# Two half-width filler products in place of each full one at the start of a two-block transformer kernel

## The chip, the core and the metric

The kernel runs on one core of one Trainium2 chip. The metric is device time in microseconds (us), the median over several executions. An execution of this kernel repeats to within half a microsecond (1849.61 to 1850.11 in three runs).

## What is computed

The reference is two transformer blocks in a row on one sequence of 256 tokens with 1024 features, all in float32. The first has a gated linear recurrence beside a latent attention, a cross attention to a memory of 256 tokens, and a gated feed-forward part. The second has a dilated and differential attention, a feed-forward part, a gated recurrent mixer (HGRN) and a mixture of eight experts of which two are chosen for each token. Only its very first step matters here:

```python
def rms_norm(x, g):
    xf = x.astype(jnp.float32)
    y = xf * lax.rsqrt(jnp.mean(xf * xf, axis=-1, keepdims=True) + EPS)
    return (y * g.astype(jnp.float32)).astype(x.dtype)
...
    h = rms_norm(x, attn_norm)
    proj = h @ w_in
```

## The kernel before

The engines' programs are written out by hand, each in one block, and meet at semaphores. The tokens lie on 128 partitions in two tiles. The weights stream from memory in units of 128 x 2048 float32 (1 MB): SyncE (SP) loads them into a ring of seven buffers `raw`, ScalarE (ACT, L1461 and L2107) rounds each to its high part `wh`, VectorE (DVE, L2225 and L3188) makes the low part `wl` as the difference, and TensorE (PE) multiplies with high and low parts (`split_product`, L425 to L436). A ring slot comes free when the low part is made; a slot of `wh` and `wl` when TensorE has used it.

The start of the program, which the change touches, goes like this.

- GpSimd (POOL) fills the tile `junk`, 128 x 512 float32, with ones (L2162) and raises `idle_columns`.
- TensorE waits for that and issues fourteen filler products (L596). Each has 128 stationary columns and 512 moving ones, all from `junk`, and writes bank 7 of `ps`. Nothing reads the result. A float32 product is run by the chip as two passes, so that the trace has 28 matmul records and 28 weight loads for the fourteen.
- In the meantime ACT sums the squares of `x` (L1481), and DVE scales its rows into `xn` (L2274), once `x` has arrived.
- TensorE then waits for `xn` and transposes it through the array (`norm`, L488), eight chunks by two tiles. ACT writes the high part of the transposed rows (L1499) and DVE the low part (L2283), both into `hT_both`. Then the first weight product starts (L425).

Every engine works strictly in the order in which its program is written: the fillers stand ahead of the transposes in TensorE's queue, ACT's rounding of weight units 1 and 2 (L1461) stands behind its part of `hT_both`, and DVE's low parts of them stand behind its own part. SP's load of the memory tokens (`mem`, L1422) waits for the transposes, and the loads of units 7 and later stand behind it.

Further on, three places of the kernel are of use for comparison. `hg_scores` (L1100) issues products with 32 or 64 stationary columns that go in turn to the lower and the upper half of the output partitions (`q0` is 0 or 64), so in turn to the two halves of the array's columns. `score` (L894, L895) issues products that contract over 32 rows only, those of successive heads in different rows of the array; at 412.5 us two heads come together, at 416.3 us one head alone. `hg_out_of` (L1134, L1140) issues products of 64 stationary columns that all go to the same half.

Of the kernel before, what the change touches and what calls it, by code (L numbers as in the profile page):

```python
# [26 lines left out]
P = 128  # L27
# [6 lines left out]
HALF = 512  # L34
# [73 lines left out]
def build(nc, units_d, consts_d, cols_d, rows_d, lru_w_d, x_d, mem_d, pos_d, out_d):  # L108
    def sb(name, shape, dt=F32):
        return nc.alloc_sbuf_tensor(name, [P] + shape, dt)  # L110
# [17 lines left out]
    junk = sb("junk", [HALF])  # L128
# [8 lines left out]
    ps = nc.alloc_psum_tensor("ps", [P, 8, HALF], F32)  # L137
# [50 lines left out]
    for shared, parts in SHARED.items():  # L188
        start = 0
# [4 lines left out]
    def sem(name):  # L194
        shared = place.get(name, (name, 0))[0]
        if shared not in sems:
            sems[shared] = nc.alloc_semaphore(shared)
        return sems[shared]
# [206 lines left out]
    def _(pe):  # L405
# [186 lines left out]


        pe.wait_ge(sem("idle_columns"), 1)
        for _ in range(14):
            nc.tensor.matmul(ps[:, 7, :], junk[:, 0:P], junk[:, 0:HALF], start=True, stop=True)  # L596
        norm("attn_norm")
        def lru_in(n, b):

# [851 lines left out]
    def _(act):  # L1451
# [352 lines left out]
        def exponentials(i):  # L1804
            _, _, _, _, _, n = score_of(i)
            act.wait_ge(*reached("dil_att_max", i + 1))
            if i >= 4:
                act.wait_ge(*reached("dil_att_transposed", (i - 4) // 2 + 1 if i < 12 else i - 7))
            p, s = apr[i % 4], asc[i % 2]
            A(p[:, 0:P], s[:, 0:P], ACT.Exp, bias=dnmax[:, n:n + 1], accum_out=dsum[:, n:n + 1])  # L1810
            A(p[:, P:], s[:, P:], ACT.Exp, bias=dnmax[:, n + 1:n + 2],
              accum_out=dsum[:, n + 1:n + 2]).then_inc(sem("dil_att_probs"), 1)
# [392 lines left out]
    def _(dve):  # L2205
# [494 lines left out]
        def biased(i):  # L2700
            _, _, _, dist, slope, n = score_of(i)
            s = asc[i % 2]
            dve.wait_ge(*reached("dil_att_scores", i + 1))
            if i >= 2:
                dve.wait_ge(*reached("dil_att_probs", i - 1))
            V.scalar_tensor_tensor(out=s, in0=dist, scalar=-slope, in1=ps[:, S_BANKS[i % 2], 0:DIST_W], op0=ALU.mult,
                                   op1=ALU.add).then_inc(sem("dil_att_read"), 1)
            dve.wait_ge(*reached("dil_att_read", i + 1))
            V.reduce_max(dnmax[:, n:n + 1], s[:, 0:P], AX, negate=True)
            V.reduce_max(dnmax[:, n + 1:n + 2], s[:, P:], AX, negate=True).then_inc(sem("dil_att_max"), 1)  # L2710
# [15 lines left out]
        def out_copied(j):  # L2726
            _, _, cs = value_of(j)
            dve.wait_ge(*reached("dil_att_weighted", j + 1))
            if j < DIFF_HEADS:
                for t in range(TT):  # L2730
                    ins = V.tensor_scalar(xn[:, t, cs], ps[:, O_BANK, 64 * t:64 * t + 64], dinv[:, 4 * j + t:4 * j + t + 1],
                                          None, ALU.mult)
            else:
                ins = V.tensor_copy(xn[:, :, cs], ps[:, O_BANK, 0:P].rearrange("p (t c) -> p t c", t=TT))
            ins.then_inc(sem("dil_att_out"), 1)
# [660 lines left out]
```

## Time and profile before

| | us |
|---|---|
| median of three runs | 1849.94 |
| lowest and highest | 1849.61, 1850.11 |
| span of the profiled execution | 1847.0 |
| first filler starts, last filler ends (TensorE) | 1.32, 15.13 |
| first transposition starts | 14.96 |

The profile is of one execution. Its span goes from the first to the last instruction on the engines. The profiled execution's own device time is not listed apart from its span; the median of the runs is 2.9 us above the span. The clock column of a stretch is TensorE's granted clock as a share of full speed, 1.00 for 2.4 GHz and 0.50 for 1.2 GHz. A matmul's duration in the records holds the way through the array, so that the time between two starts, not the duration, tells how fast passes follow each other.

### The profile page before, as it was taken

To read this page: it belongs to the slowest core of one execution; us is meant where nothing else is said; L and a number is where in the kernel's file an instruction comes from. 1 tells how busy PE (TensorE), PEld (TensorE's weight loads), DVE (VectorE), ACT (ScalarE), POOL (GpSimd) and SP (SyncE) were. 2 spreads that over 40 slices of the span, in tenths; PEclk is the share of its full clock that TensorE was granted. 3 is DMA by queue.
4 is the path that set the end of the run, shared out by engine and by line. 5 is a ranking of instruction groups with operands and counts; after the bars stand their busy time and mean duration, and the time that the engine had idled before them with its cause. 6 is when DMAs were issued, how large, how long until landed. Compare 5 with 4: busy or idle time off the path is not lost.

```text
span 1847.0 us, 24636 instructions
## 1 busy us (share of the span) xinstructions
PE 1808.2 (98%) x9274; PEld 1515.2 (82%) x9274; DVE 1502.7 (81%) x1546; ACT 1258.3 (68%) x1334; POOL 25.6 (1%) x27
## 2 busy tenths in 40 slices
PE   9989999999999999999999999999999999999997
PEld 7877788888788888987888888888888888888886
DVE  7975799568678855776988989889888889898896
ACT  6975677457655535564777777777777777777775
POOL 0000000000000000000000000000000000000000
PEclk9999999999999999999999999999999999999999
DMA  9422455543155554433799999999999999999994
GB/s 362 159 103 78 169 191 185 197 168 117 69 181 182 187 201 157 163 137 114 308 369 359 396 376 354 371 359 397 370 353 385 355 398 372 337 390 377 375 376 157
DMA packets 69087, 491.89 MB, mean 266 GB/s; under 512 B 7792, under 2 KB 8176, under 8 KB 10096
## 3 DMA queue, kind: packets, MB, share of 16 engines
q1 hardware_dynamic: 67248, 484.33, 69.0%
q0 software_dynamic: 1728, 6.03, 1.6%
q8 instruction: 76, 1.25, 0.3%
q14 instruction: 35, 0.29, 0.0%
HBM read 485.09 MB, written 5.24 MB: 265 GB/s over the span
## 4 chain that ended last, share of the span: by engine, by line
PE 90%; DVE 5%; ACT 4%; issue 1%; POOL 0%; DVEq 0%; ACTq 0%; POOLq 0%
PE ps L425 22%; PE ps L434 21%; PE ps L427 21%; PE ps L561 9%; PE ps L564 5%; PE ps L445 1%; PE ps L1381 1%; DVE wl L2225 1%; PE ps L865 1%; PE ps L866 1%; PE ps L870 1%; PE ps L436 1%; PE ps L429 1%; PE ps L1282 1%; PE ps L596 1%
## 5 line engine op out<-in xcount | busy, mean ns | idle before, releaser
L3188 DVE TENSOR_TENSOR wl<-raw,wh 128x2048 fp32r<-128x2048 f32 x334 | 761.2, 2291 | 88.2 <-ACT wh L2107 87.5
L2107 ACT ACTIVATE wh<-raw 128x2048 fp32r<-128x2048 f32 x333 | 637.9, 1918 | 182.6 <-PE ps L434 182.6
L425 PE MATMUL ps<-wh,hT_both 128*128 128x512 f32 (+2 forms) x1128 | 443.0, 394 | 5.9 <-DVE hT_both L2535 1.6
L427 PE MATMUL ps<-wh,hT_both 128*128 128x512 f32 (+2 forms) x1128 | 434.7, 386 | 0.0
L2225 DVE TENSOR_TENSOR wl<-raw,wh 128x2048 fp32r<-128x2048 f32 x124 | 283.2, 2287 | 81.8 <-ACT wh L1461 81.5
L434 PE MATMUL ps<-wl,hT_both 128*128 128x512 f32 (+2 forms) x1128 | 300.9, 386 | 0.0
L1461 ACT ACTIVATE wh<-raw 128x2048 fp32r<-128x2048 f32 x125 | 238.4, 1913 | 70.0 <-PE ps L434 68.9
L425 PE MATMUL ps<-wh,work_r 128*128 128x512 f32 x648 | 254.7, 393 | 0.0
L427 PE MATMUL ps<-wh,work_r 128*128 128x512 f32 x648 | 252.5, 390 | 0.0
L425 PEld LDWEIGHTS ps<-wh,hT_both 128*128 128x128 f32 x1128 | 212.0, 188 | 49.4 <-issue 4.5
L427 PEld LDWEIGHTS ps<-wh,hT_both 128*128 128x128 f32 x1128 | 212.1, 188 | 40.2
L434 PEld LDWEIGHTS ps<-wl,hT_both 128*128 128x128 f32 x1128 | 209.8, 188 | 42.9
L434 PE MATMUL ps<-wl,work_r 128*128 128x512 f32 x648 | 200.3, 390 | 0.6 <-DVE wl L3188 0.6
L561 PE MATMUL ps<-hT_both,wh 128*128 128x512 f32 x704 | 178.2, 394 | 2.8 <-DVE hT_both L2283 2.6
L561 PEld LDWEIGHTS ps<-hT_both,wh 128*128 128x128 f32 x704 | 126.2, 189 | 28.0 <-issue 3.0
L434 PEld LDWEIGHTS ps<-wl,work_r 128*128 128x128 f32 x648 | 121.2, 188 | 28.1 <-DVE wl L3188 2.8
L425 PEld LDWEIGHTS ps<-wh,work_r 128*128 128x128 f32 x648 | 121.7, 188 | 25.7 <-issue 1.0
L427 PEld LDWEIGHTS ps<-wh,work_r 128*128 128x128 f32 x648 | 121.7, 188 | 24.6
L564 PEld LDWEIGHTS ps<-hT_both,wl 128*128 128x128 f32 x704 | 96.1, 190 | 6.9
L564 PE MATMUL ps<-hT_both,wl 128*128 128x256 f32 x704 | 98.2, 282 | 0.0
L2117 ACT ACTIVATE work<-ps 128x512 f32<-128x512 f32 x56 | 33.5, 599 | 40.7 <-PE ps L434 40.7
L425 PE MATMUL ps<-hT_both,wh 128*128 128x256 f32 x192 | 49.2, 292 | 2.1 <-DVE hT_both L2283 2.0
(448 smaller groups left out, 1731.5 us busy)
## 6 DMA issues: line engine op xcount, KB each, us to landing
raw<-in_units SPq DMA_DIRECT2D x458, 1024.0 KB, 6.9
x<-in_x SPq DMA_DIRECT2D x2, 512.0 KB, 5.8
work<-in_lru_w SPq DMA_DIRECT2D x1, 1024.0 KB, 15.1
xn<-in_mem SPq DMA_DIRECT2D x1, 1024.0 KB, 15.6
out<-x POOLq DMA_DIRECT2D x2, 512.0 KB, 6.7
consts<-in_consts POOLq DMA_DIRECT2D x1, 768.0 KB, 5.6
consts<-in_consts SPq DMA_DIRECT2D x1, 356.0 KB, 11.5
cols<-in_cols SPq DMA_DIRECT2D x1, 202.0 KB, 2.5
```

The costliest lines, as they stand in the source:

```text
L425: nc.tensor.matmul(out, sh, mh, start=(first and j == 0), stop=False)
L427: nc.tensor.matmul(out, sl, mh, start=False, stop=False)
L429: nc.tensor.matmul(out, sh, ml, start=False, stop=False)
L434: ins = nc.tensor.matmul(out, sh, ml, start=False, stop=done)
L436: ins = nc.tensor.matmul(out, sl, mh, start=False, stop=done)
L561: nc.tensor.matmul(out, w[0][:, k, cs], hT_both[:, :, k, :], start=(k == 0), stop=False)
L564: ins = nc.tensor.matmul(out[:, 0:S], w[1][:, k, cs], hTh[:, k, :], start=False, stop=(k == KD - 1))
L1461: A(wh[:, n % SPLIT, :], raw[:, n % RAW, :], ACT.Copy).then_inc(sem("hi_made"), 1)
L2107: A(wh[:, n % SPLIT, :], raw[:, n % RAW, :], ACT.Copy).then_inc(sem("hi_made"), 1)
L2117: A(esg, ps[:, 2 * (c % 2), :], ACT.Silu).then_inc(sem("gate_silu"), 1)
L2225: V.tensor_tensor(wl[:, n % SPLIT, :], raw[:, n % RAW, :], wh[:, n % SPLIT, :].bitcast(F32), ALU.subtract).then_inc(sem("lo_made"), 1)
L3188: V.tensor_tensor(wl[:, n % SPLIT, :], raw[:, n % RAW, :], wh[:, n % SPLIT, :].bitcast(F32), ALU.subtract).then_inc(sem("lo_made"), 1)
```

## The change

Each turn of the filler loop issues two products in place of one. The first has stationary columns 0 to 63 of `junk` and writes partitions 0 to 63 of bank 7, the second has columns 64 to 127 and writes partitions 64 to 127. So each uses all 128 rows and one half of the columns of the array. The first still streams the 512 columns of `junk` in their order. The second streams the same 512 columns in another order: `by_turns` takes them alternately from the first and the second 256, that is columns 0, 256, 1, 257 and so on. All values are ones, and nothing reads the result.

```diff
         pe.wait_ge(sem("idle_columns"), 1)
+        by_turns = junk[:, 0:HALF].rearrange("p (a b) -> p b a", a=2)
         for _ in range(14):
-            nc.tensor.matmul(ps[:, 7, :], junk[:, 0:P], junk[:, 0:HALF], start=True, stop=True)
+            nc.tensor.matmul(ps[0:64, 7, :], junk[:, 0:64], junk[:, 0:HALF], start=True, stop=True)
+            nc.tensor.matmul(ps[64:P, 7, :], junk[:, 64:P], by_turns, start=True, stop=True)
         norm("attn_norm")
```

On TensorE, at the start of the program, the order before is this (a row is a line, the operation, out<-in and the output's shape; each float32 product counts once here):

```order
L404 UNCONDITIONAL_BRANCH
L596 MATMUL ps<-junk 128x512 x14
L488 MATMUL ps<-consts,xn 128x128 x16
L425 MATMUL ps<-hT_both,wh 128x256
L429 MATMUL ps<-hT_both,wh 128x256
```

And this is the beginning of it with the change:

```order
L404 UNCONDITIONAL_BRANCH
L597 MATMUL ps<-junk 64x512
L598 MATMUL ps<-junk 64x512
L597 MATMUL ps<-junk 64x512
L598 MATMUL ps<-junk 64x512
```

The pair comes fourteen times, then the sixteen transposes of L488 follow as before. No instruction of another engine, and nothing later on TensorE, is moved; later lines are numbered two higher.

## Rows read from the trace of the kernel before

**Rows 1.** The page: span, busy time by engine, and the engines' shares of the chain.

```profile
span 1847.0 us, 24636 instructions
PE 1808.2 (98%) x9274; PEld 1515.2 (82%) x9274; DVE 1502.7 (81%) x1546; ACT 1258.3 (68%) x1334; POOL 25.6 (1%) x27
...
PE 90%; DVE 5%; ACT 4%; issue 1%; POOL 0%; DVEq 0%; ACTq 0%; POOLq 0%
```

**Rows 2.** The chain that ended last, first 40 us: start, us, what.

```profile
0.74 0.54 POOL junk L2162
1.28 0.04 issue
1.32 13.81 PE ps L596 x28
15.13 0.45 PE ps L488 x4
...
15.66 3.03 ACT hT_both L1499 x8
18.70 1.81 ACT wh L1461
...
20.53 4.50 DVE wl L2225 x2
```

**Rows 3.** Timeline of DVE up to 15.4 us: start, us, engine, line, operation.

```profile
10.27 1.42 DVE L2274 TENSOR_SCALAR xn<-x,small 128x1024 f32<-128x1024 f32 x2
...
13.10 2.29 DVE L2225 TENSOR_TENSOR wl<-raw,wh 128x2048 fp32r<-128x2048 f32 x1 [1.41 <-ACT wh L1461]
```

**Rows 4.** All waits for a DMA in the whole kernel: us in total, times, longest.

```profile
DVE small L2356 <- DMA cols<-in_cols: 2.4, 1, 2.4
ACT xn L1481 <- DMA x<-in_x: 1.7, 2, 1.0
ACT wh L1461 <- DMA raw<-in_units: 1.1, 1, 1.1
```

**Rows 5.** Timeline, the fillers' weight loads (each starts with its pass) and the last filler.

```profile
2.34 0.34 PEld L596 LDWEIGHTS ps<-junk 128*128 128x128 f32 x1 [0.52 <-issue]
3.19 0.34 PEld L596 LDWEIGHTS ps<-junk 128*128 128x128 f32 x1 [0.52 <-issue]
4.05 0.34 PEld L596 LDWEIGHTS ps<-junk 128*128 128x128 f32 x1 [0.52 <-issue]
4.67 0.19 PEld L596 LDWEIGHTS ps<-junk 128*128 128x128 f32 x1 [0.28 <-issue]
5.10 0.19 PEld L596 LDWEIGHTS ps<-junk 128*128 128x128 f32 x1 [0.24 <-issue]
...
14.54 0.59 PE L596 MATMUL ps<-junk 128*128 128x512 f32 x1
14.96 0.93 PE L488 MATMUL ps<-consts,xn 128*128 128x128 f32 x7
```

**Rows 6.** Timeline of PE, 757.9 to 758.3 us: column halves in turn.

```profile
757.93 0.45 PE L1100 MATMUL ps<-work 128*32 128x32 f32 x16
```

**Rows 7.** Timeline of PE, about 412.5 and 416.3 us: two heads, then one.

```profile
412.50 0.50 PE L894 MATMUL ps<-work 32*128 32x128 f32 x4
412.82 0.60 PE L895 MATMUL ps<-work 32*128 32x256 f32 x4
413.36 0.50 PE L865 MATMUL ps<-wh,hT_both 128*128 128x512 f32 x1
...
416.34 0.48 PE L894 MATMUL ps<-work 32*128 32x128 f32 x2
416.67 0.59 PE L895 MATMUL ps<-work 32*128 32x256 f32 x2
417.19 0.39 PE L865 MATMUL ps<-wh,hT_both 128*128 128x256 f32 x1
```

**Rows 8.** Timeline of PE, 786.2 to 790 us: one half, then the whole array.

```profile
786.24 1.09 PE L1140 MATMUL ps<-work 128*64 128x128 f32 x8
787.26 0.50 PE L425 MATMUL ps<-wh,hT_both 128*128 128x512 f32 x1
...
789.21 1.07 PE L434 MATMUL ps<-wl,hT_both 128*128 128x512 f32 x4
```

**Rows 9.** Stretches: length, PE, PEld, DVE, ACT, POOL busy, granted clock, DMA share, GB/s.

```profile
866.00:870.00 4.00, 3.43 (x27) 2.15 (x25) 2.91 (x11) 3.33 (x8) 0.00 (x0) 1.00 0.74 291
...
715.00:718.00 3.00, 2.07 (x12) 1.64 (x12) 3.00 (x8) 3.00 (x7) 0.00 (x0) 0.97 0.00 0
718.00:721.50 3.50, 3.50 (x18) 3.36 (x17) 3.50 (x3) 2.80 (x6) 0.00 (x0) 0.54 0.13 23
```

**Rows 10.** Timeline of PE, 865.5 to 868.4 us: first and last of 24 eight-column products.

```profile
865.49 0.28 PE L1257 MATMUL ps<-hT_both,rh 128*8 128x256 f32 x1 [1.28 <-DVE hT_both L2283]
...
868.33 0.28 PE L1259 MATMUL ps<-hT_both,rh 128*8 128x256 f32 x1
```

## The prediction

> **What bounds the kernel now.** I read the page first: TensorE is busy for 98% of the span of 1847.0 us and holds 90% of the chain of work that ended last [rows 1]. Then I read that chain from its beginning [rows 2]. It starts with GpSimd's fill of `junk`, stays on TensorE for all 28 passes of the fillers from 1.32 us to 15.13, and goes on through the first transposes, ACT's high parts, ACT's rounding of a weight unit and DVE's low parts. So the fillers themselves are on the path. They need not be: DVE had the rows `xn` ready at 10.27 + 1.42 = 11.69 us [rows 3], and the first transpose started at 14.96, where the last filler let go [rows 5]. The fillers run about 3.3 us past the moment at which the transposes could have started. Whatever they get longer therefore delays the first transpose by the same amount, with no cover at all.
>
> Would a delay there be swallowed later? I looked for slack in the waits for DMA, since a transfer that arrives at a fixed time would absorb a shift. There are three kinds of such waits in the whole kernel, 5.2 us together, and all are over before 12 us, ahead of the first transpose [rows 4]. Behind that point every wait is of one engine for another, and all of them descend from the transposes. I take it that a shift of the first transpose reaches the end undiminished.
>
> **The change, step by step.** The loop issued 14 products, or 28 passes. It now issues 28 products of half the width, or 56 passes, and the time of a pass depends on the 512 moving columns, not on how wide the stationary part is: passes of 128 moving columns and 64 stationary ones follow each other at about (1.09 - 0.27)/7 = 0.117 us in [rows 8], where 0.27 us is the way of the last one through the array. So no half-product is cheaper than a full one. All depends on whether the two halves run at the same time.
>
> *Do the halves run together?* In [rows 6] sixteen passes of 32 moving columns go to the two column halves in turn, with different moving columns. They start (0.45 - 0.20)/15 = 0.017 us apart, again less the way through the array. By the fillers' warm rate of 0.43 us for 512 columns [rows 5], 32 columns take 0.027 us. Passes that start faster than one can stream are overlapping: one pair per 0.033 us, against 0.054 if they ran one behind the other. The row-wise counterpart is clearer, since it is longer: at 412.50 us the eight passes of two heads take 0.86 us up to the next product, and at 416.34 the four passes of one head alone take 0.85 [rows 7]. The second head is free. So I expect 28 pair-passes at the old spacing, and nothing for the doubled count.
>
> *What a pair costs beyond one pass.* The row-wise case gives 0.01 us on four pair-passes, 0.003 each. The column-wise case gives 0.033 - 0.027 = 0.006 each. I take 0.004, between the two and nearer to the row-wise one since its passes are long as the fillers are: 28 x 0.004 = 0.1 us. The ends are 0 and 28 x 0.006 = 0.17 us.
>
> *Leaving the half-width arrangement.* The full-width transposes follow directly. In [rows 8] the last half-width pass of L1140 starts at 786.24 + 1.09 - 0.27 = 787.06, and the full-width L425 starts at 787.26, 0.20 us later instead of the 0.11 that a pass of 128 columns streams. That is 0.09 us, paid once. The ends are 0 and 0.2 us, should the start of the array's new arrangement cost as much again.
>
> *The interleaved moving operand.* The second half-product reads columns 256 apart in turn, so neighbours in the stream are never neighbours in memory. No row before has such a moving operand, so I bound it. Below: nothing, or a spacing of 0.43 us per warm pass as it is. The better reason for this end is [rows 8]: the rounded weights' passes of L434 stream 512 columns every (1.07 - 0.39)/3 = 0.227 us, so contiguous elements can be delivered at nearly twice the rate at which a float32 filler pass consumes them. If jumping halves the delivery, 512 columns take 0.454 us, and the filler pass barely notices: 24 warm passes x 0.026 = 0.6 us. Above: if a float32 pass fetches its elements twice, or jumping costs more, the second half-product takes twice its time. Then a pair-pass takes 0.86 us while the clock is full, and the 24 passes from 4.67 us on give 24 x 0.43 = 10.3 us more; the first four, which ran at half clock, already have 0.85 us each. I take the lower end, nothing, since the nearest row says that the delivery has a reserve of two.
>
> The Trainium skill speaks against this step of mine. "Advanced Engine Details and Errata", section SBUF Cachelines, says that an access which goes to another 16-byte line each time pays, and that two hits on a line are wanted to hide the memory's latency. The interleaved operand never gives two hits, and the page does not say how large the penalty is; by it the sum would be somewhere from the 0.6 us to the 10.3 us above. No row here tests it. It is the first rival below.
>
> *Everything else* stays: weight loads are twice as many, but each lies beneath a pass of 0.43 us and takes 0.19 us at most with a full clock [rows 5]; the two halves write different partitions; bank 7 is read by nobody; SP, ACT, DVE and POOL have the same programs.
>
> The sum: 0.1 + 0.09 + 0 = 0.2 us. The profiled span would go from 1847.0 to 1847.2, and the median of the runs, which stands 2.9 us above the span, from 1849.94 to about **1850.2 us**, rounded up for the possible part of the interleaved operand. A measurement here can tell about 0.2%, or 3.7 us, from no change, so this is "the same". The forecast's own range is 1849.4 to 1851.5: the lower end is the scatter of the runs and a clock that happens to rise early, the upper one takes in the 0.6 us, 0.17, 0.2 and the scatter.
>
> **The rivals.**
>
> *Jumping reads are slow (chance 0.23).* Mechanism: the second product of each pair streams at half its rate, place: all warm filler passes, price 24 x 0.43 = 10.3 us, and it decides from the point at which jumping delivers less than one element in 0.84 us (0.43/512). Time 1849.9 + 10.3 + 0.2 = **1860.4, slower**. For it: the rule above, and that the one moving operand made so is new here. Against it: the reserve of two. A lesser slowing, of a third, would give 3.4 us.
>
> *The halves do not overlap at 512 columns (0.05).* Then 56 passes run one behind the other. The clock rises at the same time, so about four passes lie ahead of 4.67 us and 52 behind it: 4.67 + 52 x 0.43 = 27.0 us instead of 14.96, or +12.0, **1862**. Against it: [rows 6, 7].
>
> *The clock does not rise during half-width products (0.05).* Now it does so between the passes at 4.05 and 4.67, where the spacing falls from 0.85 to 0.43 us [rows 5]. If it stayed at half until other work comes, 24 passes would cost 0.43 us more each, 10.3 us, and the first transposes would be slow too: **1861**. Against it: 24 products with as few as 8 stationary columns, almost back to back from 865.49 to 868.33 us [rows 10], go by at a granted clock of 1.00 [rows 9]; the one drop to about half, at 718 us, follows a stretch in which TensorE stood idle for a third of the time [rows 9]. A rise later by one or two passes would cost under 1 us and stays inside "the same".
>
> *The fillers get shorter (0.02).* If the clock rose right at the first pass, the first four would save 0.43 us each, 1.7 us: 1848.2, still no more than 0.1%. For a gain beyond 3.7 us the pair would have to run faster than a single product, which no row suggests.
>
> **How the numbers follow.** The forecast has 0.65, and the small saving 0.02. The three slow rivals have 0.33 together, nearly all at +10 to +12 us. Of the jumping reads' 0.23 about 0.01 would be too small to be told from no change. Faster by over 0.2%: 0.02, the most that I leave for what I have not seen. Same: 0.66. Slower: 0.32. Since the slow cases hold a third, a range for 8 times in 10 has to reach them: it goes from 1849.2 to 1862.2. With a third of the cases at its far end, the predicted time stays that of the likeliest.
>
> **What would show it.** Right: in the new profile the fillers start at 1.32 us as before, the records of the two lines come in pairs that start a few nanoseconds apart, successive pairs 0.85 us apart at first and 0.43 from about 4.7 us on, and the first transpose starts at 15.0 to 15.3. Wrong by jumping reads: the spacing stays near 0.85 us although the granted clock is 1.00, or the second record of a pair lasts longer than the first, and the first transpose starts near 25 us. Wrong by the clock: the same spacing at a granted clock of 0.50. Wrong by missing overlap: the records of L597 and L598 start 0.43 us apart from each other, and the transposes start near 27. Wrong on the path: the transposes start late, but the span does not grow by as much.

## The result, and the profile after

The changed kernel took 1852.76 us (median of 18 runs, 1850.99 to 1853.66), the kernel before 1849.66 us (median of 18, 1847.44 to 1851.76). The ratio is 1.0018 with a 95% interval of 1.0011 to 1.0026. So the change costs about 3.1 us, which lies on the border of what I had called "the same": the interval lies above 1, so the kernel did become slower, and it reaches to both sides of my bound of 0.2%. The scatter is wider than the three first runs had suggested, some 4 us between the extremes of the kernel before and not half a microsecond.

The changed kernel's page, its first lines, beside [rows 1]:

```profile
span 1851.9 us, 24692 instructions
...
PE 1814.9 (98%) x9302; PEld 1519.0 (82%) x9302; DVE 1502.4 (81%) x1546; ACT 1258.0 (68%) x1334; POOL 25.5 (1%) x27
```

56 instructions more are the 28 additional passes and their weight loads. DVE and ACT have the same busy time as before. The place to look is the chain's beginning, beside [rows 2]; here is its piece from the end of the fillers on (start, us, what):

```profile
16.14 2.33 PE ps L598 x5
18.47 0.60 PE ps L488 x4
...
19.16 3.02 ACT hT_both L1501 x8
```

ACT's high parts start at 19.16 in place of 15.66, 3.5 us late. The links after the fillers are the same as before. The end of the fillers in the chain is five passes of L598 alone, the interleaved half. The timeline of TensorE shows how that comes about; first while the array runs at half clock, then at full clock, then at the end (start, us, what):

```profile
3.94 1.06 PE L597 MATMUL ps<-junk 128*64 128x512 f32 x1
3.95 1.05 PE L598 MATMUL ps<-junk 128*64 128x512 f32 x1
4.79 1.06 PE L597 MATMUL ps<-junk 128*64 128x512 f32 x1
4.80 1.05 PE L598 MATMUL ps<-junk 128*64 128x512 f32 x1
...
6.32 0.59 PE L597 MATMUL ps<-junk 128*64 128x512 f32 x1
6.38 0.71 PE L598 MATMUL ps<-junk 128*64 128x512 f32 x1
6.75 0.59 PE L597 MATMUL ps<-junk 128*64 128x512 f32 x1
6.92 0.71 PE L598 MATMUL ps<-junk 128*64 128x512 f32 x1
7.18 0.59 PE L597 MATMUL ps<-junk 128*64 128x512 f32 x1
7.46 0.70 PE L598 MATMUL ps<-junk 128*64 128x512 f32 x1
...
15.07 1.07 PE L597 MATMUL ps<-junk 128*64 128x512 f32 x2
15.61 2.87 PE L598 MATMUL ps<-junk 128*64 128x512 f32 x5
18.41 0.44 PE L488 MATMUL ps<-consts,xn 128*128 128x128 f32 x2
```

Three things are to be read here. At half clock the two halves start 0.01 us apart and the pairs follow each other every 0.85 us, as single products did. At full clock L597 goes on at 0.43 us from pass to pass (6.32, 6.75, 7.18), but L598 takes 0.54 (6.38, 6.92, 7.46), and it falls behind: the two halves do not wait for each other, up to a lead of four or five passes. The last two passes of L597 came 0.60 and 0.48 us after the one before, so that a limit on the lead is possible; no run tests it. At the end L597 is done (at 16.14 us) and L598 runs its last passes alone, (2.87 - 0.71)/4 = 0.54 us each. The first transpose starts at 18.41 instead of 14.96, which is 3.45 us.

The clock rose later in this execution than in the one before: the spacing falls to the full-clock value after 5.64 us instead of after 4.05. (The granted clock column reads 1.00 up to the first recorded change, so that only the spacing tells.) By the clock's own records it rose at 6.1 and 4.4 us, and 1.7 us at half speed cost 0.85 of those 3.45. About 22 full-clock passes x 0.112 = 2.5 us and 0.09 us for the way back to full width are the rest. A median over 18 runs does not hang on one execution's clock, so the slow half-product was the suspect for the 3.1 us, and there were two further candidates to clear: the sharing of the array, and the clock.

### The profile page after: what moved, and what is told of

Its sections match the earlier page's. It is cut to its first block, busy times and chain, and to the rows that moved or that the text cites. A ratio compares the mean times of both kernels' runs of the same rounds, so it can differ in the third digit from the quotient of the medians.

```text
span 1851.9 us, 24692 instructions
## 1 busy us (share of the span) xinstructions
PE 1814.9 (98%) x9302; PEld 1519.0 (82%) x9302; DVE 1502.4 (81%) x1546; ACT 1258.0 (68%) x1334; POOL 25.5 (1%) x27
## 4 chain that ended last, share of the span: by engine, by line
PE 90%; DVE 5%; ACT 3%; issue 1%; POOL 0%; DVEq 0%; ACTq 0%; POOLq 0%
PE ps L425 22%; PE ps L434 21%; PE ps L427 21%; PE ps L561 9%; PE ps L564 5%; PE ps L445 1%; PE ps L1383 1%; PE ps L867 1%; DVE wl L2227 1%; PE ps L868 1%; PE ps L872 1%; PE ps L436 1%; PE ps L1284 1%; PE ps L429 1%; ACT wh L1463 1%
## 5 line engine op out<-in xcount | busy, mean ns | idle before, releaser
L434 PE MATMUL ps<-wl,hT_both 128*128 128x512 f32 (+2 forms) x1128 | 300.9, 386 | 0.0
L434 PEld LDWEIGHTS ps<-wl,hT_both 128*128 128x128 f32 x1128 | 209.8, 188 | 42.9
L434 PE MATMUL ps<-wl,work_r 128*128 128x512 f32 x648 | 200.4, 390 | 0.5 <-DVE wl L3190 0.5
L434 PEld LDWEIGHTS ps<-wl,work_r 128*128 128x128 f32 x648 | 121.1, 188 | 28.2 <-DVE wl L3190 2.8
```

Of the source, the lines that this page charges most:

```text
L434: ins = nc.tensor.matmul(out, sh, ml, start=False, stop=done)
```

## The experiments

In all of them only the filler loop of the kernel before is edited (and nothing reads what it computes), unless said. A diff shows the whole edit against the kernel before. The comparison is with the kernel before, run on the same chip. The theories: A, the order of reading costs, whoever reads beside it; B, two streams at once starve each other; C, half-width products delay the clock's rise.

**Both halves in memory order.**

```diff
-            nc.tensor.matmul(ps[:, 7, :], junk[:, 0:P], junk[:, 0:HALF], start=True, stop=True)
+            nc.tensor.matmul(ps[0:64, 7, :], junk[:, 0:64], junk[:, 0:HALF], start=True, stop=True)
+            nc.tensor.matmul(ps[64:P, 7, :], junk[:, 64:P], junk[:, 0:HALF], start=True, stop=True)
```

> Both half-products of each pair stream the 512 columns in memory order; nothing else differs from the change. Theory A (the reading order costs: an interleaved moving operand streams 512 float32 columns in 0.54 us in place of 0.43, whoever reads beside it): both halves go at 0.43 us per pass at full clock, the first transpose starts at 15.0 to 15.3 us when the clock rises at about 4.4 us (0.43 us later for each microsecond by which it rises later), and the time is within 0.5 us of the kernel before, about 1849.9. Theory B (contention: two streams at once starve each other, whatever their order): the second half stays at 0.54 us per pass, transposes near 18, time near 1852.8. Theory C (half-width products delay the rise of the clock): the spacing falls to 0.43 only after 6 us again, and the time is about 0.9 us above the kernel before.

Measured: 1849.97 us (11 runs) against 1849.65, ratio 1.0001 (0.9992 to 1.0010). The end of the fillers in its timeline:

```profile
13.74 0.59 PE L596 MATMUL ps<-junk 128*64 128x512 f32 x1
13.74 0.59 PE L597 MATMUL ps<-junk 128*64 128x512 f32 x1
...
14.60 0.59 PE L596 MATMUL ps<-junk 128*64 128x512 f32 x1
14.60 0.59 PE L597 MATMUL ps<-junk 128*64 128x512 f32 x1
15.12 1.09 PE L488 MATMUL ps<-consts,xn 128*128 128x128 f32 x8
```

The pairs are in step, two of them in 0.86 us, as single products were. The doubled number of products is free. The transposes follow the last pair after 0.52 us where a pass takes 0.43: the way back to full width costs the 0.09 us of the forecast. A transpose at 15.12 and a span of 1847.0 us, that of the kernel before, speak against B, and C falls too, since the clock had risen by the pass at 4.72 us.

**Full-width products, interleaved.**

```diff
+        by_turns = junk[:, 0:HALF].rearrange("p (a b) -> p b a", a=2)
         for _ in range(14):
-            nc.tensor.matmul(ps[:, 7, :], junk[:, 0:P], junk[:, 0:HALF], start=True, stop=True)
+            nc.tensor.matmul(ps[:, 7, :], junk[:, 0:P], by_turns, start=True, stop=True)
```

> Fourteen full-width fillers as before, but each streams its 512 columns interleaved (0, 256, 1, 257 and so on). Theory A: 24 warm passes at 0.54 us, the first transpose about 2.6 us later than before, near 17.6, and the time about 2.7 us above the kernel before, like the changed kernel. Theory B: there is one stream only, so passes stay at 0.43 us and the time at 1849.7. Theory C: the clock rises at about 4.4 us, time as before.

Measured: 1852.49 us (9 runs) against 1849.65, ratio 1.0022 (1.0012 to 1.0032).

```profile
16.11 1.78 PE L597 MATMUL ps<-junk 128*128 128x512 f32 x3
17.73 0.82 PE L488 MATMUL ps<-consts,xn 128*128 128x128 f32 x6
```

Passes are (1.78 - 0.70)/2 = 0.54 us apart with a single stream, and the first transpose starts at 17.73, 2.77 us after that of before at nearly the same rise of the clock. So nearly the whole price of the change, 2.8 of 3.1 us in the medians, comes without any half-width product. A holds.

**Both halves interleaved.**

```diff
+        by_turns = junk[:, 0:HALF].rearrange("p (a b) -> p b a", a=2)
         for _ in range(14):
-            nc.tensor.matmul(ps[:, 7, :], junk[:, 0:P], junk[:, 0:HALF], start=True, stop=True)
+            nc.tensor.matmul(ps[0:64, 7, :], junk[:, 0:64], by_turns, start=True, stop=True)
+            nc.tensor.matmul(ps[64:P, 7, :], junk[:, 64:P], by_turns, start=True, stop=True)
```

> Both half-products of each pair stream interleaved. Theory A: both at 0.54 us per pass, in step with each other, and the same time as the changed kernel, 1852.8. Theory B or a mixture (two jumping streams meet in the same memory): a spacing above 0.54 us, up to 0.86, and a time from 1853 to 1860.

Measured: 1853.45 us (11 runs) against 1849.65, ratio 1.0018 (1.0009 to 1.0027).

```profile
6.50 1.02 PE L597 MATMUL ps<-junk 128*64 128x512 f32 x1
6.51 1.01 PE L598 MATMUL ps<-junk 128*64 128x512 f32 x1
7.36 0.70 PE L597 MATMUL ps<-junk 128*64 128x512 f32 x1
7.36 0.71 PE L598 MATMUL ps<-junk 128*64 128x512 f32 x1
7.90 0.70 PE L597 MATMUL ps<-junk 128*64 128x512 f32 x1
7.90 0.71 PE L598 MATMUL ps<-junk 128*64 128x512 f32 x1
```

Two jumping streams run in step at 0.54 us: no extra price for the second. The time alone would not have told: 1853.45 lies in the range that I had given to a mixture with B, 0.7 us above the changed kernel's median; but the ratios of the two are the same, 1.0018, and the spacing decides. At half clock, up to 6.50, the interleaved passes take 0.85 us like any other. In this execution the clock rose only at 7.35 us.

**Ten fillers, and eighteen.** Full width, memory order; `range(10)` and `range(18)` in place of `range(14)`. Ten asks whether there is a gain, eighteen whether a delay reaches the end.

> Ten full-width fillers in memory order in place of fourteen: 8 passes or 3.4 us less. Expected if the fillers stand on the path as the chain has it: they end at about 11.7 us, when the scaled rows are ready, ACT's high parts start at 13.1 (behind its rounding of the first weight unit) in place of 15.7, DVE's low parts at 15.4 (behind its low part of the first unit) in place of 16.5, and the time is 1.2 to 2.0 us below the kernel before, about 1848. Rival: a later stage absorbs the shift, and the time is as before. Rival: with fewer fillers the clock is lost again in the early products, and the time is above the kernel before.

> Eighteen full-width fillers in memory order in place of fourteen: 8 warm passes of 0.429 us, 3.43 us more ahead of the transposes, and nothing else. If a delay there reaches the end undiminished, the time is 3.4 us above the kernel before, about 1853.1, somewhat above the changed kernel, whose fillers let go 2.8 us late at the same rise of the clock. If a later stage swallows part of a delay, the time is less than 2.5 us above the kernel before, and then the changed kernel's 3.1 us must have another source than its fillers.

> The same kernel as the one with ten fillers, for a narrower interval. If it is faster at all, the two sets of runs together give a median 0.4 to 1.2 us below the kernel before; if the first difference was scatter, this one lies within 0.3 us of it.

Eighteen: 1853.01 us (11 runs) against 1849.49, ratio 1.0018 (1.0009 to 1.0027). The chain starts like this:

```profile
1.32 17.14 PE ps L596 x36
...
19.00 3.03 ACT hT_both L1499 x8
```

3.43 us of plain fillers in order, and 3.5 us at the end. The delay arrives undiminished, within the scatter. The changed kernel's 3.1 us agree with the delay of about 2.8 us in its fillers; the interval of the ratio, 2.0 to 4.8 us, can't tell the two apart.

Ten: 1848.91 us (11 runs) against 1849.65, and again 1848.63 (11 runs) against 1849.83, both times with a ratio of 0.9995 (0.9986 to 1.0004). Both medians are lower, by 0.7 and 1.2 us, and both intervals reach above 1, so that neither set by itself excludes no change. The 22 executions together have a median of 1848.85 us, against 1849.65 of the 45 of the kernel before that were measured beside them: 0.8 us less, which lies in the 0.4 to 1.2 that I had named for a real gain. By the means it is 1.0 us with a standard error of 0.3, if each execution counts as independent. So a small gain is likely, and it is smaller than the 1.2 to 2.0 us expected at first.

One reason is in the chain, which no longer holds the fillers. In the first profile it goes over the transfer of a weight unit, ACT's rounding and DVE's low part of it (start, us, what):

```profile
3.10 8.51 DMA raw<-in_units
```

Four fillers less end 3.43 us earlier, but less of that can be gained, since the first weight unit is now what is waited for. In this execution the clock also rose late, at 7.4 us, the first transpose started at 13.02 us and ACT's high parts at 13.72, 1.9 us earlier than before, yet its span is 1848.0 us. Another reason is visible in the stretches (length, PE, PEld, DVE, ACT, POOL busy, granted clock, DMA share, GB/s):

```profile
13.00:17.60 4.60, 2.74 (x22) 2.32 (x21) 4.03 (x6) 4.42 (x10) 0.00 (x0) 1.00 1.02 425
17.60:21.00 3.40, 3.40 (x17) 3.40 (x17) 3.40 (x5) 2.75 (x2) 0.00 (x0) 0.51 1.00 424
21.00:25.00 4.00, 4.00 (x35) 4.00 (x35) 3.79 (x10) 0.80 (x3) 0.00 (x0) 0.99 1.01 426
```

TensorE ran 3.4 us at half clock and gave part of the gain back. The stretch ahead of it, with TensorE busy for 2.74 of 4.60 us, does not explain that: in the second profile of the same kernel it was busy for less, and no such drop followed.

```profile
13.00:17.60 4.60, 2.19 (x17) 1.72 (x14) 4.52 (x7) 4.60 (x10) 0.00 (x0) 1.00 1.01 423
```

The clock had risen at 5.3 us there, and the span was 1848.0 us as well, with four half-clock stretches of 3.4 us further on, where the profile of the kernel before has one. What makes them come is open.

**Eight fillers**, `range(8)`.

> Eight full-width fillers: 12 passes or 5.1 us less than before. They end at 9.9 to 11.3 us, ahead of the scaled rows at 11.7, so that the transposes start at about 11.9. The chain then goes over ACT's rounding of the first weight unit, which lasts to 13.1 us: ACT's high parts start there at the earliest, as with ten fillers. Expected 1.0 to 2.0 us below the kernel before, no better than ten fillers. Rival: the shorter warm stretch makes half-clock stretches in the first products likelier, each of 3.4 us costing up to 1.7 us, and the time is that of the kernel before or above.

Measured: 1848.89 us (11 runs) against 1849.49, ratio 0.9995 (0.9986 to 1.0004). The transposes start at 11.69 us, released by `xn`. The clock rose at 6.9 us and fell to half from 17.1 to 20.5, as in the first profile of ten. A small gain is possible and not shown, and none of these versions beats the kernel before clearly.

**Which orders cost.** Full-width float32 fillers: five in memory order, then two products, or four passes, of each order.

```diff
-        for _ in range(14):
-            nc.tensor.matmul(ps[:, 7, :], junk[:, 0:P], junk[:, 0:HALF], start=True, stop=True)
+        straight = junk[:, 0:HALF]
+        steps = [straight.rearrange("p (b a) -> p a b", a=n) for n in (2, 4, 8, 16)]
+        turns = [straight.rearrange("p (a b) -> p b a", a=n) for n in (2, 4)]
+        for moving in [straight] * 5 + [m for m in steps + turns for _ in range(2)]:
+            nc.tensor.matmul(ps[:, 7, :], junk[:, 0:P], moving, start=True, stop=True)
```

> One look, no timing: full-width fillers that stream the same 512 float32 columns, first five in memory order, then two products each with a step of 2, 4, 8 and 16 elements (sweeping the 512 in as many passes over them), then two each alternating between 2 and between 4 places (256 and 128 apart). If what costs is that no two neighbours of the stream lie in one 16-byte line, step 2 stays at 0.43 us per pass and all the others take 0.54. If any order but memory order costs, step 2 takes 0.54 as well. If the cost grows with the distance, step 16 and the alternating ones take more than step 4.

There is one execution of it, of 1859.17 us with a span of 1857.4. A pass's successor loads its weights as the pass starts, so the starts of the weight loads give the spacing. Of each order two neighbours (memory order, step 2, step 4, step 8, step 16, two places, four places):

```profile
6.57 0.19 PEld L599 LDWEIGHTS ps<-junk 128*128 128x128 f32 x1 [0.24 <-issue]
7.00 0.19 PEld L599 LDWEIGHTS ps<-junk 128*128 128x128 f32 x1 [0.24 <-issue]
...
8.33 0.19 PEld L599 LDWEIGHTS ps<-junk 128*128 128x128 f32 x1 [0.26 <-issue]
8.78 0.19 PEld L599 LDWEIGHTS ps<-junk 128*128 128x128 f32 x1 [0.26 <-issue]
...
11.01 0.21 PEld L599 LDWEIGHTS ps<-junk 128*128 128x128 f32 x1 [0.69 <-issue]
11.91 0.21 PEld L599 LDWEIGHTS ps<-junk 128*128 128x128 f32 x1 [0.69 <-issue]
...
13.72 0.21 PEld L599 LDWEIGHTS ps<-junk 128*128 128x128 f32 x1 [0.71 <-issue]
14.64 0.21 PEld L599 LDWEIGHTS ps<-junk 128*128 128x128 f32 x1 [0.71 <-issue]
...
18.20 0.21 PEld L599 LDWEIGHTS ps<-junk 128*128 128x128 f32 x1 [0.65 <-issue]
19.05 0.21 PEld L599 LDWEIGHTS ps<-junk 128*128 128x128 f32 x1 [0.65 <-issue]
...
21.01 0.19 PEld L599 LDWEIGHTS ps<-junk 128*128 128x128 f32 x1 [0.35 <-issue]
21.55 0.19 PEld L599 LDWEIGHTS ps<-junk 128*128 128x128 f32 x1 [0.35 <-issue]
...
22.95 0.21 PEld L599 LDWEIGHTS ps<-junk 128*128 128x128 f32 x1 [0.67 <-issue]
23.82 0.21 PEld L599 LDWEIGHTS ps<-junk 128*128 128x128 f32 x1 [0.67 <-issue]
```

In us per pass of 512 float32 columns: 0.43 in memory order, 0.45 at a step of 2 elements (8 bytes), 0.90 at 4 (16 bytes), 0.92 at 8, 0.85 at 16, 0.54 between two places, 0.87 between four. My expectation that every order without neighbours in a line costs 0.54 was wrong: a steady step of 16 bytes or more doubles the time, and the changed kernel's alternation of two places is the cheap special case. The span confirms the path once more, at a mean clock of 0.997 like the kernel before: the transposes started 10.6 us late, and the span grew by 10.4.

**Other types.** Six plain float32 fillers, then bfloat16 views of `junk`, and after the transposes fp32r products from the first unit's high part.

```diff
+        def look(one):
+            for turned in (False, True):
+                moving = one[:, 0:HALF].rearrange("p (a b) -> p b a", a=2) if turned else one[:, 0:HALF]
+                for _ in range(8):
+                    nc.tensor.matmul(ps[:, 7, :], one[:, 0:P], moving, start=True, stop=True)
+
-        for _ in range(14):
+        for _ in range(6):
             nc.tensor.matmul(ps[:, 7, :], junk[:, 0:P], junk[:, 0:HALF], start=True, stop=True)
+        look(junk[:, 0:HALF].bitcast(mybir.dt.bfloat16))
         norm("attn_norm")
+        pe.wait_ge(sem("hi_made"), 1)
+        look(wh[:, 0, 0:HALF])
```

> One look, no timing: after six plain float32 fillers, eight bfloat16 products of 512 columns in memory order and eight interleaved (a step of 512 bytes); and after the transposes, eight products each of the rounded float32 kind (fp32r, as the weights have it), in memory order and interleaved. A float32 pass of 512 columns takes 0.43 us and interleaved 0.54; fp32r and bfloat16 in order should take 0.22. If delivery of jumping elements is limited to one in 1.05 ns (0.54 us for 512), both take 0.54 us interleaved, two and a half times as long. If a float32 pass fetches everything twice, the limit is one in 0.53 ns and both take 0.27. If the penalty is a fixed 0.11 us per pass, both take 0.33.

Its time, 1848.75 us in one run, means nothing, as fillers and products differ in number. The bfloat16 passes take 0.22 us in order (nine loads in 1.82 us, below) and 0.48 interleaved, with a step of 512 bytes between the two places:

```profile
8.15 1.82 PEld L599 LDWEIGHTS ps<-junk 128*128 128x128 bf16 x9 [0.33 <-issue]
10.36 0.10 PEld L599 LDWEIGHTS ps<-junk 128*128 128x128 bf16 x1 [0.38 <-issue]
10.84 0.10 PEld L599 LDWEIGHTS ps<-junk 128*128 128x128 bf16 x1 [0.39 <-issue]
```

The fp32r ones, first the group in order, then the interleaved one:

```profile
15.41 2.09 PE L599 MATMUL ps<-wh 128*128 128x512 f32 x8
...
17.34 1.89 PE L599 MATMUL ps<-wh 128*128 128x512 f32 x8
```

With last passes of 0.39 and 0.38 us, eight starts lie (2.09 - 0.39)/7 = 0.24 and (1.89 - 0.38)/7 = 0.216 us apart. For fp32r interleaving costs nothing. None of my three readings foresaw that, and none has bfloat16 at 0.48 either; the nearest was 0.54. The next kernel was to tell whether the first group had only been disturbed by what other engines did beside it:

```diff
-        for _ in range(14):
+        def look(one, orders):
+            row = one[:, 0:HALF]
+            for order in orders:
+                moving = {"line": row, "turns": row.rearrange("p (a b) -> p b a", a=2),
+                          "step 4": row.rearrange("p (b a) -> p a b", a=4), "step 8": row.rearrange("p (b a) -> p a b", a=8)}[order]
+                for _ in range(6):
+                    nc.tensor.matmul(ps[:, 7, :], one[:, 0:P], moving, start=True, stop=True)
+
+        for _ in range(5):
             nc.tensor.matmul(ps[:, 7, :], junk[:, 0:P], junk[:, 0:HALF], start=True, stop=True)
+        look(junk[:, 0:HALF].bitcast(mybir.dt.bfloat16), ("line", "step 4", "step 8"))
         norm("attn_norm")
+        tile_ready(KD - 1)
+        pe.wait_ge(sem("hi_made"), 1)
+        look(wh[:, 0], ("turns", "line", "step 4", "turns", "line"))
```

> One look, no timing. Six bfloat16 products each in memory order, at a step of 4 elements (8 bytes) and at a step of 8 (16 bytes); after the transposes, with the low and high parts of the rows complete, six fp32r products each in the orders interleaved, memory order, step of 4 (16 bytes), interleaved, memory order, all from the first unit's high part. If two neighbours in one 16-byte line are what counts, bfloat16 takes 0.22 to 0.25 us at a step of 4 and more than 0.43 at a step of 8. For fp32r: if its passes are free of the penalty, all five groups take 0.22 to 0.23; if the earlier look hid it, because other engines touched the same tile during the straight passes, the interleaved groups are again at 0.216 and a step of 4 is at 0.45 or more.

One execution, of 1863.01 us. Passes of bfloat16 took 0.22 us in order, 0.45 at a step of 8 bytes and 0.90 at 16 bytes, so a step of 8 bytes doubled the time where I had expected next to nothing. The first two groups of fp32r fell for the most part into a stretch at half clock and are left out. The other three, at step 4 (16 bytes), interleaved, and in order:

```profile
28.50 2.02 PE L601 MATMUL ps<-wh 128*128 128x512 f32 x4
...
30.79 1.03 PE L601 MATMUL ps<-wh 128*128 128x512 f32 x4
...
31.89 1.09 PE L601 MATMUL ps<-wh 128*128 128x512 f32 x4
```

With passes of 0.64, 0.38 and 0.39 us that is (2.02 - 0.64)/3 = 0.46, (1.03 - 0.38)/3 = 0.217 and (1.09 - 0.39)/3 = 0.233 us from start to start. So fp32r is not free of the price of a 16-byte step, and is free of that of two alternating places. One thing is not taken apart here: the fp32r passes read the tile `wh` with real weights in it, the float32 and bfloat16 ones read `junk` with ones in it. That the difference comes from the type and not from the tile is the likelier reading, and no run tests it.

## Why the range held the time and the sum was too small

**What bounds the kernel: right.** The fillers were on the path with no cover, and a delay reached the end undiminished: 3.43 us of plain fillers gave 3.5 in the medians, and with the six orders a first transpose 10.6 us late gave 10.4 in the span. The few waits for DMA, all early [rows 4], had told that, and the changed kernel's profile has the same three kinds and no other.

**Do the halves run together: right.** L597 and L598 start 0.01 us apart, and two halves in order take what one full product took. The sixteen short passes of [rows 6] and the row-wise case [rows 7] were enough to see it.

**What a pair costs beyond one pass:** forecast 0.1 us over all, measured nothing that shows (pairs at 0.43 us).

**Leaving the half-width arrangement: right**, 0.09 us, to the hundredth as read off [rows 8].

**The interleaved moving operand: this step failed.** I took nothing, "since the nearest row says that the delivery has a reserve of two". The term is 24 full-clock passes x 0.112 = 2.7 us. It lies between the two ends I had kept, 0 (or 0.6) and 10.3 us. With it the sum is 2.7 + 0.09 = 2.8 us, against a measured 3.1; full-width interleaved fillers alone gave 2.8. The rest is within the scatter of the medians, in which the clock's rise between 4.2 and 7.4 us has its part: each microsecond by which it is late costs fillers in memory order half of one.

Why did the row mislead? The reserve came from L434, an fp32r pass [rows 8], and I applied it to a plain float32 pass. The runs show that the two kinds of pass, on their two tiles, do not fare alike: the same interleaving costs fp32r nothing and float32 26%, while at a step of 16 bytes both double, 0.23 to 0.46 and 0.43 to 0.90. A float32 pass costs about two fp32r passes in order and at that step (0.43 to 0.23, 0.90 to 0.46), as if it went over its operand twice; the forecast had named that possibility for its upper end. But it costs two and a half of them when interleaved (0.54 to 0.217), so "twice over" does not explain it all. That part stays open, and with it why the alternation costs what it does. What the runs show is the price of each order.

The Trainium skill's rule, in "Advanced Engine Details and Errata", section SBUF Cachelines, was the better guide here: it had the sign right for this operand. In these runs a step of 2 float32 elements, which leaves two neighbours in each 16-byte line, costs 5%, and a step of 4, which leaves none, 110%. The interleaved operand, which leaves none either, costs float32 only 26% and fp32r nothing, and bfloat16 at a step of 8 bytes, which does leave two, costs 109%; these depart from the rule as I read it, and there the measurement decides.

**The rivals.** "Jumping reads are slow" had the place and the direction, and one of its signs showed (the second record of a pair lasts longer, 0.71 to 0.59 us); its price was too high: it doubled the pass where 26% was true. I had named 3.4 us for a lesser slowing, which was nearly it, but gave it no weight of its own; the error of form was to let two ends stand for a quantity that can take any value between them. Missing overlap fell with the halves in order. That half-width products delay the clock's rise is not borne out: it came at 6.1 us with the change, at 4.6 with two halves in order and at 7.35 with both interleaved, but also anywhere from 4.2 to 7.4 with full-width fillers. The medians leave little room for it, as two halves in order stand 0.3 us above single products, with a ratio of 1.0001.

**The number.** 1850.2 was forecast and 1852.8 measured, inside the whole range of 1849.2 to 1862.2 and outside the forecast's own 1849.4 to 1851.5. "The same" holds only as narrowly as the interval of 0.11% to 0.26% says, and that it holds at all is in part luck: the term put at nothing came out at 2.7 us, just under the 3.7 that I had taken as the bound. The wide range held the time because of rivals at 10 to 12 us that did not come true. Two slips of the forecast change nothing in this: the break-even of jumping reads is one element in 0.84 nanoseconds, not microseconds (the interleaved float32 pass came to 1.05), and the small saving's chance of 0.02 was counted under faster, although 1848.2 us would have been the same.

## What to carry to other kernels

Products that use only half of the array's columns and go to the other half in turn run side by side at no cost that shows, even with moving data in different orders and at different speeds; a switch back to full width costs about 0.1 us. Look at the order in which a moving operand is read before anything else: a stride of 16 bytes doubled a pass of float32 and of fp32r and made one of bfloat16 four times as long (0.22 to 0.90 us), and 8 bytes, nearly free for float32, doubled bfloat16. And when a price is taken from the nearest row, check that the row is of the same data type: a bound from another type is not a bound.

## What was not expected of the hardware

- The two halves of the array keep no step with each other. The half in memory order went on at 0.43 us a pass beside one at 0.54, until it was four to five passes ahead, and finished 2.3 us earlier.
- Two alternating places are far cheaper than a steady step (0.54 against 0.90 us for float32), and four alternating places are not (0.87). For bfloat16 two places cost about as much as a step of 8 bytes (0.48 and 0.45). For fp32r they are even slightly faster than memory order, 0.217 to 0.233 us, in both kernels that tried it.
- At half clock the interleaved order costs nothing: 0.85 us a pass in either order. A limit near 0.54 us that does not follow TensorE's clock would be hidden under these 0.85; that fits, and is not shown.
- The clock's first rise lay anywhere from 4.2 to 7.4 us in the twelve profiled executions, and with it up to 1.6 us of the fillers' length. Half-clock stretches at other places come and go as well; the profile of the changed kernel had one of 3.4 us at 105 us and one of 6.8 at 201 that the one of before had not, which goes with a span 4.9 us longer where the medians are only 3.1 apart.
